# Turning the rows behind an expert stage in two halves of the tokens

## The reference

```
x = x + hier_moe(h, ...)            # experts' sums added to the residual
x = rms_norm(x, final_norm)         # end of the first block
xn = rmsnorm(x, pre_mix_norm)       # start of the second
proj = xn @ w_in                    # 2720 columns: rq 512, rk 512, rv 512, rg 512, ...
rq = rope(rq, positions); rk = rope(rk, positions) * (RET_HEAD_DIM ** -0.5)
```

## Time and profile before

| | us |
|---|---|
| median of three runs | 2045.78 |
| lowest and highest | 2044.46, 2045.87 |
| the profiled execution, its own time | 2043.54 |
| its span in the trace | 2041.7 |
| TensorE busy | 1766.9 (87%) |
| VectorE busy | 902.2 (44%) |
| ScalarE busy | 739.2 (36%) |
| GpSimd busy | 265.8 (13%) |

### The profile page before, as it was taken

The page is one execution under the profiler, slowest core; times in us unless marked ns, Lnnn a source line. Parts: engine busy times, 40 slices in busy tenths (PEclk is TensorE's granted clock), DMA queues, the critical chain, the costliest instruction groups (busy, mean ns, idle before and its releaser), DMA issues.

```text
span 2041.7 us, 37869 instructions
## 1 busy us (share of the span) xinstructions
PE 1766.9 (87%) x15190; PEld 1274.1 (62%) x15190; DVE 902.2 (44%) x1699; ACT 739.2 (36%) x1382; POOL 265.8 (13%) x281
## 2 busy tenths in 40 slices
PE   7999999787777777787778678779989999999998
PEld 5677787544444444444434444358867789998877
DVE  5555335533222322222232223266275698886245
ACT  4444522232222222322222222253365554445143
POOL 0000000000000000000000000640010078880000
PEclk9999999899989988989898999889999999999999
DMA  6222232699999999999999999944230233333222
GB/s 209 78 83 71 75 103 95 274 366 422 427 426 426 426 425 427 425 428 425 427 425 427 426 426 427 423 143 118 84 86 10 73 96 119 107 104 121 96 83 83
DMA packets 109058, 506.17 MB, mean 248 GB/s; under 512 B 9480, under 2 KB 59016, under 8 KB 75696
## 3 DMA queue, kind: packets, MB, share of 16 engines
q1 hardware_dynamic: 100864, 492.07, 60.5%
q10 hardware_dynamic: 6512, 8.94, 1.7%
q0 software_dynamic: 1600, 4.02, 0.8%
HBM read 497.32 MB, written 2.11 MB: 245 GB/s over the span
## 4 chain that ended last, share of the span: by engine, by line
PE 61%; DMA 29%; DVE 6%; ACT 2%; issue 2%; SPq 1%; ACTq 0%; DVEq 0%
DMA ring<-in_w 28%; PE bank L686 13%; PE bank L687 13%; PE bank L688 13%; PE bank L2569 8%; PE bank L2481 4%; PE bank L2560 3%; PE bank L874 2%; PE bank L900 1%; PE bank L886 1%; SPq L2115 1%; PE bank L2578 1%; DMA raw<-in_w_in 1%; PE bank L1221 1%; DVE w_lo L791 0%
## 5 line engine op out<-in xcount | busy, mean ns | idle before, releaser
L2569 PE MATMUL bank<-ring,XTs 128*32 128x256 f32 x4032 | 286.3, 428 | 111.8 <-DMA ring<-in_w 109.0
L2823 DVE TENSOR_TENSOR x<-x,bank 128x512 f32<-128x512 f32 x264 | 163.8, 681 | 483.9 <-PE bank L2560 483.2
L2569 PEld LDWEIGHTS bank<-ring,XTs 128*32 128x32 f32 x4032 | 154.5, 120 | 245.4 <-issue 183.5
L2578 PE MATMUL bank<-ring,aT 128*32 128x256 f32 x2048 | 124.5, 383 | 90.4 <-DVE aT L2843 90.4
L2348 ACT ACTIVATE y<-bank 32x256 f32<-32x256 f32 x256 | 96.1, 375 | 227.2 <-PE bank L2560 140.8
L686 PE MATMUL bank<-hTh,w_hi 128*128 128x512 f32 x362 | 146.1, 404 | 5.8 <-DVE hTl L838 3.5
L791 DVE TENSOR_TENSOR w_lo<-raw,w_hi 128x2048 fp32r<-128x2048 f32 (+4 forms) x47 | 96.5, 2059 | 120.7 <-ACT w_hi L775 120.6
L2578 PEld LDWEIGHTS bank<-ring,aT 128*32 128x32 f32 x2048 | 66.7, 110 | 129.2 <-issue 96.8
L2481 PE MATMUL bank<-arena,oh 128*32 128x256 f32 x2048 | 143.3, 418 | 4.3 <-DVE oh L2805 0.8
L687 PE MATMUL bank<-hTh,w_lo 128*128 128x512 f32 x362 | 143.1, 395 | 0.0
L688 PE MATMUL bank<-hTl,w_hi 128*128 128x512 f32 x362 | 142.2, 393 | 0.0
(11 more groups left out here) (467 smaller groups left out, 3687.4 us busy)
## 6 DMA issues: line engine op xcount, KB each, us to landing
ring<-in_w SPq DMA_DIRECT2D x190, 2048.0 KB, 19.6
raw<-in_w_in SPq DMA_DIRECT2D x25, 1024.0 KB, 5.5
late_raw<-in_w_gate SPq DMA_DIRECT2D x11, 1024.0 KB, 5.3
late_raw<-in_w_up SPq DMA_DIRECT2D x11, 1024.0 KB, 5.4
late_raw<-in_w_down SPq DMA_DIRECT2D x11, 1024.0 KB, 5.0
raw<-in_w_out SPq DMA_DIRECT2D x4, 1024.0 KB, 5.1
third<-in_w SPq DMA_DIRECT2D x2, 2048.0 KB, 23.0
raw<-in_w_o SPq DMA_DIRECT2D x4, 1024.0 KB, 5.2
```

The source lines that it names most:

```text
L2569: mm = pe.matmul(Hb[BLK * j:BLK * (j + 1), :], XTs[u][:, 4 * (c % 2) + 2 * h + c // 2, :], w[:, at_:at_ + Q], start=(h == 0 and c == 0), s ...
L2578: mm = pe.matmul(Yb[BLK * j:BLK * (j + 1), :], aT[:, r, h, :], ring[3 * u + 2][:, at_:at_ + Q], start=(h == 0 and r == 0), stop=(h == 1 an ...
L2823: ins = v.tensor_tensor(xs, xs, Sb[t % 2][n][:, :], ALU.add)
```

## The change

`hT3`, the turned rows, becomes two sets of four banks, both in banks 0 to 3. A set holds 256 tokens, and a bank of it two chunks of columns with 256 tokens each. The four banks of `rq` are 4 to 7.

TensorE (`pe_second`) does for each half h: turn two tiles into the four banks; for the first half, wait for the last `flush`; then compute for all four banks of `rq` the columns of this half, 96 matmuls with 256 moving columns. `rq`'s banks are filled only in the second half, so both units of weights stay in use until then. ScalarE rounds one weight unit ahead instead of two, and does the first two tiles up to the scaled rows, two banks of columns, the second unit, and then the third and fourth tile among the rest. VectorE likewise adds and norms two tiles, makes the low part of the first unit, adds the other two tiles, and mixes the norms and the second unit with the columns of the first half.

```diff
-        plan("hT3", DC)
-        plan("rq", RH, "each")
+        J["hT3"] = [bk.take(4, range(4))]
+        J["rq"] = bk.take(RH, range(4, 8))
+        J["hT3"].append(bk.take(4, range(4)))
+        ends("rq")
+        bk.next = 0
...
-            pe_to_feature(pe, J["hT3"], lambda i, c: xn4(i)[:, P * c:P * (c + 1)], lambda i: pe.wait_ge(S("xn4"), i + 1))
-            pe_feature(pe, "rq", hT, fresh="hT3")
+            for h in range(2):
+                for job in J["hT3"][h]:
+                    claim(pe, job)
+                for i in (2 * h, 2 * h + 1):
+                    pe.wait_ge(S("xn4"), i + 1)
+                    for j, job in enumerate(J["hT3"][h]):
+                        for c, dst, _ in half_chunks(h, j):
+                            mm = pe.transpose(dst[:, P * (i % 2):P * (i % 2 + 1)], xn4(i)[:, P * c:P * (c + 1)], ident)
+                        if i % 2:
+                            fill(mm, job)
+                if h == 0:
+                    sums_left()
+                half = slice(Q * h, Q * (h + 1))
+                for k, job in enumerate(J["rq"]):
...
+                        mm = three(pe, banks[job.bank][:, half], (wh[:, c, cols], wl[:, c, cols]),
+                                   (hTh[:, c, half], hTl[:, c, half]), c == 0, c == DC - 1)
+                    if h:
+                        fill(mm, job)
...
-            hi_until(act, n_first + 1)
+            hi_until(act, n_first)
...
+            squares(0)
+            squares(1)
+            rows_out(0)
+            rows_out(1)
+            columns_hi(0, 0)
+            columns_hi(0, 1)
+            hi_until(act, n_first + 1)
+            squares(2)
+            columns_hi(0, 2)
+            squares(3)
+            columns_hi(0, 3)
+            rows_out(2)
+            rows_out(3)
...
+            for j in range(4):
+                columns_hi(1, j)
...
-            act_split_jobs(act, "hT3", hTh, lambda c: mix_gain[:, c:c + 1])
...
+            last_sums(0)
+            last_sums(1)
+            both_norms(0)
+            both_norms(1)
+            inverse(0)
+            inverse(1)
+            lo_until(v, n_first)
+            last_sums(2)
+            last_sums(3)
+            columns_lo(0, 0)
+            columns_lo(0, 1)
+            both_norms(2)
+            lo_until(v, n_first + 1)
+            columns_lo(0, 2)
+            both_norms(3)
+            columns_lo(0, 3)
+            inverse(2)
+            inverse(3)
...
+            for j in range(4):
+                columns_lo(1, j)
...
-            dve_split_jobs(v, "hT3", hTh, hTl, lambda c: mix_gain[:, c:c + 1])
```

More of the change, by code:

```diff
@@ L1196, in sums_of, with half_chunks, pe_second @@
             return [banks[job.bank][:, Q * h:Q * (h + 1)] for h in range(2)]
-        def pe_second(pe):
-            pe_to_feature(pe, J["hT3"], lambda i, c: xn4(i)[:, P * c:P * (c + 1)], lambda i: pe.wait_ge(S("xn4"), i + 1))
-            pe_feature(pe, "rq", hT, fresh="hT3")
+        def half_chunks(h, j):
+            bank = banks[J["hT3"][h][j].bank]
+            return [(2 * j + k, bank[:, Q * k:Q * (k + 1)], slice(Q * h, Q * (h + 1))) for k in range(2)]
+        def pe_second(pe, sums_left):
+            for h in range(2):
[12 more added lines that the diff above has]
+                for k, job in enumerate(J["rq"]):
+                    u = units_of["rq"][k // 2]
+                    wh, wl = parts(u)
+                    if h == 0:
+                        if k % 2 == 0:
+                            loaded(pe, u)
+                        claim(pe, job)
+                    cols = slice(P * (k % 2), P * (k % 2 + 1))
+                    for c in range(DC):
+                        if k == 0 and c % 2 == 0:
+                            read(pe, [J["hT3"][h][c // 2]])
+                        mm = three(pe, banks[job.bank][:, half], (wh[:, c, cols], wl[:, c, cols]),
+                                   (hTh[:, c, half], hTl[:, c, half]), c == 0, c == DC - 1)
+                    if h:
+                        fill(mm, job)
             pe_feature(pe, "rk", hT)
@@ L2365, in rows_out, with squares, columns_hi @@
                 act.activation(xn4(i), x[:, i, :], ACT.Copy, scale=rstd2[:, i:i + 1]).then_inc(S("xn4"), 1)
-            for i in range(NT):
+            def squares(i):
                 act.wait_ge(S("x2pre"), i + 1)
                 act.activation(xg(i), x[:, i, :], ACT.Square, accum_out=ssq[:, i:i + 1]).then_inc(S("tile_squares"), 1)
-                if i >= 2:
-                    rows_out(i - 2)
-            rows_out(NT - 2)
-            rows_out(NT - 1)
+            def columns_hi(h, j):
+                full(act, J["hT3"][h][j])
+                for c, src, half in half_chunks(h, j):
+                    act_split(act, ("hT3", h, c), hTh[:, c, half], src, mix_gain[:, c:c + 1])
+            squares(0)
[11 more added lines that the diff above has]
+            rows_out(3)
             act.sem_inc(S("norm_squares"), 1)
+            for j in range(4):
+                columns_hi(1, j)
             act_sqrt(act, "n3", rstd, NT)
             act.dma_start(scratch[:, 0:2048], a["decays"]).then_inc(S("w_dec"), 16)
-            act_split_jobs(act, "hT3", hTh, lambda c: mix_gain[:, c:c + 1])
             act_second(act, chain, row)
@@ L2648, in _, with left, sums_left @@
                 scatter(count + 1, t)
-            pe.wait_ge(flushed, 4 * count + 14)
-            for job in J["before_moe"]:
-                pe.sem_inc(filled[job.bank], 1)
-                pe.sem_inc(freed[job.bank], 1)
-            pe_second(pe)
+            def left(jobs):
+                for job in jobs:
+                    pe.sem_inc(filled[job.bank], 1)
+                    pe.sem_inc(freed[job.bank], 1)
+            def sums_left():
+                pe.wait_ge(flushed, 4 * count + 14)
+                left([job for job in J["before_moe"] if job.bank >= 4])
+            left([job for job in J["before_moe"] if job.bank < 4])
+            pe_second(pe, sums_left)
         @block.vector
@@ L2870, in inverse, with last_sums @@
                 v.reciprocal(rstd2[:, i:i + 1], rstd2[:, i:i + 1]).then_inc(S("n34"), 1)
-            for t in range(NT):
+            def last_sums(t):
                 flush(count + 1, t)
```

11 lines of the change are left out of this document (5 added, 6 removed).

## The result

| | us |
|---|---|
| before, median of 4 runs (range) | 2045.12 (2044.41 to 2045.87) |
| changed, median of 4 runs (range) | 2058.37 (2056.04 to 2060.27) |
| ratio, 95% interval | 1.0062 [1.0049, 1.0074] |
| forecast (range) | 2053.3 (2050.0 to 2057.0) |

The change makes the kernel some 13 us slower: the forecast had the sign, and a little over half of the size (7.5 of 13.3 us). The profiled run of the changed kernel took 2060.27 and is the slowest of its four; the profiled run of before took 2043.54. The two traces differ by 16.8 us, some 3.5 more than the medians.

What follows compares the result with a forecast made beforehand. TensorE, idling at the seam until rq, was taken to pass rq's delay on one for one: 3.6 + 9.4 + 1.5 + 3.1 + 11.6 less 22.06 is +7.1; with 0.4 for rk +7.5, so 2053.3 us (2050.0 to 2057.0).

Steps and rivals of the forecast that it cites:

- VectorE up to the first half's columns: At the seam before rq: VectorE's list completes the first half's columns at 1358.5; all tokens' low parts previously ended at 1359.5.
- 78 narrow matmuls and the width: rq's first half: 78 matmuls after 1358.6 at 0.12 us take 9.4 us; halving the columns costs 1.0 over rq.
- The clock: rq's first half: the unbroken row from 1358.6 begins at half clock for 3.0 us, costing +1.5 us.
- Between the halves: Between rq's halves: sixteen transposes, high part, low part and first matmul stand open, 3.1 us; scaled rows cost nothing.
- rq's end: End of rq on TensorE: 1384.2 against 1377.1 before, +7.1 us.
- Behind rq ... I take +0.4: rk's weight units after rq: first just fits, second needed as made at 1395.2; +0.4 us, between 0 and 3.
- GpSimd's own delay costs nothing: Behind rq: GpSimd starts some 22 us later at no cost, since x is wanted only beyond 1420.
- rk starves: Rival, 16%: GpSimd stretches the low part of rk's first unit or the angles; 2 to 3 us more, +10, 2055.8.
- The rival of the ideal overlap: Rival, 6%: VectorE has banks 2 and 3 before 1353.7, rq ends at 1377.0, no change, 2045.8.

Runs made afterwards that it cites:

- columns_late: pool_late with all four banks of the first half's columns made before the third and fourth tiles' norms and second weight unit, on ScalarE and VectorE: 2045.58 us.
- again: The changed kernel measured and profiled once more, unchanged: 2056.10 us, ratio 1.0062.
- pool_late: The changed kernel with GpSimd's eight residual operations held back until the low part of rk's second unit is made: 2050.19 us.
- warm_pool: pool_late with 46 idle transposes in the four waits before and between the first half's first matmuls: 2050.72 us.
- lo_first: The changed kernel with VectorE making the low part of rk's second unit before the rotation angles instead of behind them: 2051.41 us.
- turn_best: turn_warm with the low part of rq's second unit and the third tile's reciprocal pulled ahead of the last norm on VectorE: 2042.05 us, ratio 0.9988.
- turn_warm: columns_late with the second half's transposes before the first half's last bank, and ten idle transposes ahead of rq's first matmul: 2044.35 us.
- width: The kernel before with each bank of rq as two times 24 matmuls of 256 columns, old bank order: 2046.63 us, ratio 1.0005.

## Why the prediction was right in sign and short in size

- **VectorE up to the first half's columns: right.** 1358.5 forecast, 1358.0 measured, each piece in its place (bank 0 at 1349.5, banks 2 and 3 behind a norm each). *columns_late* confirms that this order is the main loss ahead of rk: undone, rk comes 5.0 us sooner.
- **78 narrow matmuls and the width: right to a few tenths.** The width is 0.6 rather than 1.0. By the estimate from the Trainium skill ("TensorE: Matmul & The Clock Gate", section "Back-to-back issue gap") it would have been 0.2; the measurement lies midway between the two.
- **The clock: the mechanism right, the size too small in the profiled run.** The half level lasted 5.3 us of the unbroken row (1358.04 to 1363.3) and not the 3.0 of the row before: the 78 matmuls took 11.7 us, 2.5 more than at 0.118 each, where 1.5 was forecast. In *again* it is 1.6 or 1.7, with 16 slow distances for 25, and in *pool_late* 1.8; *warm_pool* took away 1.7. The price differs by 0.9 us between two executions of one program, and the forecast's bounds for it, 0 to 1.5, end too low.
- **Between the halves: right.** Sixteen transposes at 1369.73, first matmul at 1372.82: 3.09 for 3.1. The third and fourth rows were ready 9 us early (1360.8 for 1369.7), where 8 were forecast.
- **rq's end: right.** Forecast 1384.2; without the wait ahead of rk it would have been 1384.3. That it is right to 0.1 is partly luck: the clock took 1.0 more than forecast, and the columns, the narrow matmuls and the second half some 0.9 less.
- **"Behind rq ... I take +0.4": this is the step that failed.** It was mis-sized: 6.0 us were measured (0.95 + 3.38 + 1.7), and 5.6 in *again*. It had taken the low part of rk's first unit at the duration of a row without a neighbour, 2.3, where it took 3.86, and the angles at the 9.5 us of the earlier trace rows, where they took 12.4. Of those 9.5 the first seven instructions lay beside GpSimd, whose work ended at 1379.73, and the last two did not, 0.43 each; these two are what grew, to 3.7 us. The forecast itself wrote that GpSimd would now lie beside "the whole of them", and that the slack was nought. The trace had the prices: the low part of rk's first unit took 2.72 there beside GpSimd, ending 2.14 behind its TENSOR_TENSOR, and angle instructions beside it took 1.24, 1.34 and 2.52 where twins take 0.43 to 0.49. (Only one of them took some 2 us more than its twin, L1056; the forecast's rival says two. Three others took 0.8 more.) As an estimate from such rows: GpSimd's first three operations (2.4, 2.85 and 2.4 us) behind the second half's columns end at about 1383.0, so the low part ends at 1385.2, 1 us behind the need at 1384.2. Its bound of 3 us ("all angles as slow as the first ones") was close to the 2.9 by which the angles grew, but it left out the unit ahead of them, 1.6, which moves them, and what the resulting wait does to the clock, 1.7, which the forecast did not price at all. *pool_late* (5.9 us less by moving GpSimd alone) shows the cause, and *lo_first* (4.7 less) that the order on VectorE is its other half.
- **"GpSimd's own delay costs nothing": wrong in effect.** Nobody waits for its result, true; what costs is where it runs.
- **The rival "rk starves"** was this mechanism, with the right place, at 16% and at 2 to 3 us more than the forecast. It should have been the forecast, with 6. The rival of the ideal overlap was priced rightly, level, as far as *columns_late* stands for it (that kernel also has GpSimd moved).
- **The remainder**, 3.1 us of the profiled run beyond rk, is for 2.9 a stretch at half level that the kernel before has in one of its two profiles, and every other kernel here has. No run ties it to a step of the change.
- **Left open**: why the clock fell after TensorE had resumed from rk's wait, and not during it; why GpSimd stretches some instructions of VectorE and leaves others of the same form alone; and which of the five parts of *turn_best* its gain can spare. No run took them out one by one.

## What to carry to other kernels

When a change delays the point at which GpSimd starts, find what VectorE has to do in the new place, and do not price it by a row without GpSimd, or by a sum over a mixture. Lay the two engines' operations side by side and look which one is running when the other begins; the same low part took from 2.28 to 4.33 us here. A slack shorter than the GpSimd operation beside it (up to 2.4 us here) counts as none. Starting work earlier by halves did not pay here until the first half's operands were made in one piece and the second half's turn lay inside the first half's matmuls; with both it was level, and a gain of 2 us took two more steps. Moving work that nobody waits for behind the operands that somebody waits for costs one wait, and was worth 6 us here.

## What the runs showed of the hardware

- **GpSimd beside VectorE slows some instructions of VectorE, and not others of the same shape.** A low part of 128x2048 takes 2.47 to 4.33 us instead of 2.29 when it begins beside GpSimd's TENSOR_TENSOR, and ends 2.14 to 2.16 behind it, in twenty of twenty cases. A TENSOR_SCALAR on 128x512 takes 2.51 instead of 0.43 there, and ends 0.28 behind it. GpSimd's own TENSOR_SCALAR on 128x1024 goes from 2.85 to 4.76, so both sides pay. Beside GpSimd's TENSOR_SCALAR some angle instructions stay at 0.43 or 0.69 and others take 0.8 more; what decides that was not settled.
- **A wait of 3.4 us in the middle of an unbroken row cost 1.7 us again behind it**: the granted clock was 1.00 during it and until 1400.8, and 0.50 from 1401.5 to 1403, after TensorE had resumed at 1399.88. In *again* it fell within 0.6 us of the resumption, at the same cost. Behind waits of 0.6 to 1.2 us at the start of rq's second half and of rk the matmuls stayed at the full level's distance.
- **Ten idle transposes in a gap that is idle anyway brought the full clock for the first matmuls** (*turn_warm*), and 46 of them 1.7 us by the landmarks (*warm_pool*). At the half level narrow matmuls lie 0.21 us apart, at the full one 0.12.
- **The full level is not one tempo.** The kernel before, profiled twice, had its wide matmuls 0.229 and 0.234 us apart, both at a granted clock of 1.00: 0.4 us over rq.
- **Halving the columns of a matmul whose operands are still being made** costs far more than its width: 2.1 us for the first 24 in *width*, because TensorE overtakes the engine that feeds it.
